# Output projection of a gated-linear mixer with tokens as rows and its layer norm along rows

## The chip, the cores and the metric

One core of one Trainium2 chip runs the whole program in one launch. The metric is the device time in microseconds (us); of several executions the median is given. The engines are TensorE (PE), VectorE (DVE), ScalarE (ACT) and GpSimd (POOL); SyncE (SP) issues the loads of weights.

## What is computed

Batch 1, 256 tokens, width 1024, three mixers and a feed-forward in a first block, then a second block of two layers. The change lies in the second block:

```python
def second_block(x, ...):
    for layer in range(DEPTH_2):
        if layer < N_A_LAYERS:
            y = gla_mixer(x, ...)
        else:
            k_sh, v_sh = shared_kv(x, w_kv)
            y = dilated_mixer(x, ..., k_sh, v_sh)
        x = layer_norm(DEEPNORM_ALPHA * x + y, ln_g[layer], ln_b[layer])
    return x

def gla_mixer(x, w_in, w_a2, b_a2, norm_g, w_out):
    ...
    return (o.astype(x.dtype) * jax.nn.silu(g)) @ w_out

def layer_norm(x, g, b):
    mu = jnp.mean(x32, axis=-1, keepdims=True)
    xc = x32 - mu
    var = jnp.mean(xc * xc, axis=-1, keepdims=True)
    return xc * lax.rsqrt(var + LN_EPS) * g + b
```

Everything is fp32. `ALPHA` is the square root of 2.

## The kernel before, in words

The weights stream from HBM as some 100 chunks of 1 MB, each 1024 rows by 256 columns, in an order fixed by constants: ..., `GG` (4 chunks, the gate of the gated-linear mixer), `GOUT` (4, its output projection), `SK` (3, shared keys), `SV` (3), `SWA` (16, queries and gate of the last mixer), `SOUT` (4, the last projection). SP loads a chunk into one of four raw buffers when its former occupant has been split. ScalarE writes the chunk's rounded high half (`high`), VectorE the remainder (`low`, L997), into one of three buffer pairs, once the chunk three before has been multiplied. PE makes each product as three fp32r products: high by high, low by high, high by low (`three`, L1544 to L1546), 48 of 256 columns for one chunk.

Activations lie with features on the partitions: `x`, `xe`, `tb`, `hhi`, `hlo` are [128, 8, 256], eight blocks of 128 features by 256 tokens. Weights are then the stationary operand (`fm`), and a result bank holds two blocks of features for all tokens. `fm_first` interleaves two chunks over k, so that PE has work while its inputs still arrive. In `SV` and `SOUT` the activations are stationary and the result has tokens as rows.

Each engine runs its own list of instructions in order, with semaphores between them. For every chunk b its list holds the work on the chunk's result and the split of chunk b+3; for the chunks in `LATE` the split comes after all the other work. `RESULT_DRAIN` says by whose count a result bank (three, used in turn) is free again, `CHUNK_MARK` when a chunk has been multiplied.

Around `GOUT` before: VectorE adds each result bank to `xe` (ALPHA times the input of the layer, with features on partitions, made by POOL). After two of four chunks PE takes the mean of those 512 features by products with a matrix of 1/1024 (`shift_mean`), and VectorE subtracts twice that mean. ScalarE squares, POOL adds squares, PE sums them over partitions (`sums`, `rest_mean`, `last_squares`) and then makes 16 warm-up products of the identity (`warm`, L1592). VectorE corrects the mean, finds the root and scales the eight blocks (L1430); ScalarE rounds them to `hhi` with the bias (L657), VectorE writes `hlo` (L1033), POOL two of the blocks. Then SK starts. During `SV`, POOL makes ALPHA times the normed x for the last residual.

Around `SOUT` before: PE adds the last residual itself, by 16 products of a 128x128 block of `x` with the identity (L1934) in front of the real products. ScalarE copies the banks to `z` with row sums (L909, L921), takes squares about a provisional mean with row sums (L916, L922), and VectorE ends the norm along rows (L1452 to L1468) for each tile t of 128 tokens: row scalars in `zs`, parameters repeated on all partitions in `ln_rows`. The first 512 features of a tile give the provisional mean.

Of the kernel before, what the change touches and what calls it, by code (L numbers as in the profile page):

```python
# [89 lines left out]
def results_of(c):  # L90

    if BRANCH <= c < WOUT:
        return 4
    if DOWN <= c < GK:
        return 2 if (c - DOWN) % 3 == 2 else 0
    return 1


def drainer_of(c):

    if c < MISC or BRANCH <= c < WOUT or (UP <= c < DOWN and (c - UP) % 2 == 1):
        return "dve"
    if GOUT <= c < SV or SWA <= c < SWA + 12:
        return "dve"
    return "act"
# [15 lines left out]
for _c in range(NC):  # L121
# [8 lines left out]
    CHUNK_MARK.append(_m)  # L130

# [73 lines left out]
def build(nc, xT, crow_d, cols_d, ident_d, rope1_d, rope2_d, amask_d, cmask_d, tri_d, dmask_d, sel_d, rel_d, w_a2_d,  # L205
          w_ada, wts, ln_rows_d, out_d):
# [3 lines left out]
    with ctx:  # L210
# [17 lines left out]
        ident = sb("ident", [P, P])  # L228
        meanw = sb("meanw", [P, P])
# [37 lines left out]
        result_rows = y[:, :, :].rearrange("p a b -> p (a b)").rearrange("p (t n) -> p t n", t=2)  # L267
        xsw = sq[:, 0:2, :]
# [17 lines left out]
        with ExitStack() as st:  # L286
            xe = sb("xe", [P, KT, T], at=st)
            gq = sb("gq", [P, 4, T], at=st)
            gk = sb("gk", [P, 4, T], at=st)
            alrT = sb("alrT", [16, T], at=st)  # L290
            wa2 = sb("wa2", [16, 512], at=st)
            keep = sb("keep", [P, 1024], at=st)
            cum = sb("cum", [P, 1024], at=st)
            qI = sb("qI", [P, 1536], at=st)
# [7 lines left out]
            with ExitStack() as early:  # L302
                gfacs = sb("gfacs", [P, 4096], at=early)
            gohi = sb("gohi", [P, KT, T], f32r, at=st)
            golo = sb("golo", [P, KT, T], f32r, at=st)
            grs = cum[:, :].rearrange("p (h t) -> p h t", h=4)
# [5 lines left out]
        with ExitStack() as st:  # L312
# [14 lines left out]
            zs = sb("zs", [P, 2, 16], at=st)  # L327
# [10 lines left out]
        rest = pX[:, T:2 * T]  # L338
        msq = pS[:, 0:T]
# [13 lines left out]
        NORMS = ("n1", "n2", "n3", "n4", "n5")  # L353
# [6 lines left out]
        centered, summed = {"n5": sem("n5_centered")}, {"n5": sem("n5_summed")}  # L360
        rows_in, z_shift, z_summed, z_squared, z_var, z_root = (
            sem(n) for n in ("rows_in", "z_shift", "z_summed", "z_squared", "z_var", "z_root"))
        shift_known, rest_squared, var_known, recentered = (
            sem(n) for n in ("shift_known", "rest_squared", "var_known", "recentered"))
        in_lo_pool = {n: sem(f"{n}_lo_pool") for n in ("n3", "n5")}
# [124 lines left out]
        def _(pool):  # L490
# [34 lines left out]
            def presum(n, need):  # L525

                for i in range(2):
                    a = 2 * i + 2
                    pool.wait_ge(squares[n], need[i])
                    if i:  # L530
                        pool.wait_ge(presummed, 2 * ("n2", "n4", "n5").index(n) + 1)
# [11 lines left out]
            for c in range(1, NC + 1):  # L543
# [14 lines left out]
                if c - 1 == SK - 1:  # L558
                    presum("n5", (2, 3))
                    split_lo_pool("n5", x, lambda i: col("ln_b", i))  # L560
                if SV <= c - 1 < SWA:
                    pool.wait_ge(scaled["n5"], KT)
                    rest = [i for i in range(KT) if i not in LO_POOL]
                    for k in rest[2 * (c - 1 - SV):2 * (c - 1 - SV) + 2]:
                        nc.gpsimd.tensor_scalar(x[:, k, :], tb[:, k, :], col("ln_b", k), ALPHA, ALU.add, ALU.mult
                                                ).then_inc(x_ready, 1)
                    if c - 1 == SWA - 1:
                        pool.wait_ge(in_lo_pool["n5"], 2)
                        for k in LO_POOL:
                            nc.gpsimd.tensor_scalar(x[:, k, :], x[:, k, :], ALPHA, None, ALU.mult).then_inc(x_ready, 1)  # L570
# [32 lines left out]
        def _(act):  # L603
# [38 lines left out]
            def norm_guess(n, eps):  # L642

                if n not in centered:
                    act.wait_ge(mean_known[n], 1)
                else:
                    act.wait_ge(var_known, 1 if n == "n5" else 2)
                var = logvar[:, :] if n in centered else stat
                nc.scalar.activation(rstd[:, :], var, ACT.Abs_reciprocal_sqrt, bias=col(eps, 0)).then_inc(guess_known, 1)
# [22 lines left out]

            TAIL = 3
            for c in range(1, NC + 1):
# [4 lines left out]
                if b not in LATE and b != WOUT + 2:  # L679
# [214 lines left out]
                if GOUT < b < SK:  # L894
                    n, j = "n5", b - GOUT
                    for i in ((), (0, 1), (2,), (3,))[j]:
                        act.wait_ge(centered[n], i + 1)
                        nc.scalar.activation(sq[:, 2 * i:2 * i + 2, :], tb[:, 2 * i:2 * i + 2, :], ACT.Square
                                             ).then_inc(squares[n], 1)
                    if j == 2:  # L900
                        load_root()
                if b == SK - 1:
                    norm_guess("n5", "eps5")
                    split_hi("n5", tb, lambda k: col("ln_b", k))
                if SOUT <= b < SOUT + 2:
                    j = b - SOUT
                    ps = result(FIRST_RESULT[b])
                    for t in range(2):
                        nc.scalar.activation(z[:, t, T * j:T * j + T], ps[:, T * t:T * t + T], ACT.Copy,  # L909
                                             accum_out=zs[:, t, j:j + 1]).then_inc(drained_act if t else act_self, 1)  # L910
# [1140 lines left out]
```

## Time and profile before

| | |
|---|---|
| median of 3 runs | 795.97 us (795.43 to 796.54) |
| the profiled execution's own time | 794.63 us |
| its span | 792.8 us |
| PE, DVE, ACT, POOL busy | 93%, 68%, 50%, 15% of the span |
| products of GOUT | 558.33 to 583.53 us |
| products of SK to SWA | from 593.73 us |
| products of SOUT | 761.18 to 784.83 us |

Times inside are microseconds from the start of the span. A row of a timeline gives start, length, engine, line of the kernel, operation, output<-inputs, shapes and count, and in brackets the idle time before it and what ended it. PE's products overlap: their starts tell the pace. An fp32 product (identity, mean) leaves two records, an fp32r product or a transpose one.

### The profile page before, as it was taken

The page shows a single profiled execution, that of the slowest core. Times are in us where ns is not written, and L with a number is a line of the kernel's source. Part 1 is how long each engine was busy: PE and PEld are TensorE (multiplying, and loading weights), DVE is VectorE, ACT ScalarE, POOL GpSimd, SP SyncE. Part 2 cuts the span into 40 slices and gives each one's busy share as a digit, 9 for nine tenths or more (in the row PEclk, how much of TensorE's full clock was granted, in tenths as well). Part 3 has the DMA queues.
Part 4 walks back from the last instruction along what each step waited for, and adds up shares of the span by engine and source line. Part 5 has one row for each costly group of instructions (what it writes and reads, how often), then busy time and mean ns, then how long its engine had stood idle before and what let it go on. Part 6 is the DMA issues. An engine that isn't in the chain of part 4 may idle for free. (4 is left out here: it accounts for less than half of the span.)

```text
span 792.8 us, 14332 instructions
## 1 busy us (share of the span) xinstructions
PE 738.1 (93%) x6028; PEld 722.6 (91%) x6028; DVE 536.8 (68%) x777; ACT 397.3 (50%) x549; POOL 121.2 (15%) x100
## 2 busy tenths in 40 slices
PE   2499999999898999999999999999989999999996
PEld 2399989989898999999999999999989999999995
DVE  4968987675868777777756556926686547556544
ACT  3165645555344554544444337718535556555633
POOL 0030000000421100000001160000025755433000
PEclk9699999999999999999999999979999999999998
DMA  9964656565445256555556614632345653333101
GB/s 353 416 245 174 243 188 258 184 242 212 160 149 223 61 206 212 191 183 177 216 222 236 216 58 164 209 107 93 126 155 208 211 204 117 129 130 111 51 1 54
DMA packets 21096, 140.62 MB, mean 177 GB/s; under 512 B 2372, under 2 KB 3012, under 8 KB 5032
## 3 DMA queue, kind: packets, MB, share of 16 engines
q1 hardware_dynamic: 20600, 137.80, 47.8%
q0 software_dynamic: 432, 1.90, 0.6%
q8 instruction: 48, 0.79, 0.4%
q14 instruction: 16, 0.13, 0.0%
HBM read 138.64 MB, written 1.05 MB: 176 GB/s over the span
## 5 line engine op out<-in xcount | busy, mean ns | idle before, releaser
L1544 PE MATMUL res<-hhi,whi 128*128 128x256 f32 (+1 forms) x1168 | 336.7, 288 | 7.2 <-DVE hlo L1033 5.1
L997 DVE TENSOR_TENSOR wlo<-raw,whi 128x2048 fp32r<-128x2048 f32 (+1 forms) x105 | 236.8, 2257 | 145.9 <-ACT whi L620 141.3
L1545 PE MATMUL res<-hhi,wlo 128*128 128x256 f32 (+1 forms) x1168 | 331.0, 283 | 0.0
L1546 PE MATMUL res<-hlo,whi 128*128 128x256 f32 (+1 forms) x1168 | 331.0, 283 | 0.0
L620 ACT ACTIVATE whi<-raw 128x2048 fp32r<-128x2048 f32 (+1 forms) x105 | 195.8, 1867 | 137.1 <-issue 108.3
L1544 PEld LDWEIGHTS res<-hhi,whi 128*128 128x128 f32 (+1 forms) x1168 | 223.4, 191 | 9.5 <-issue 4.7
L1545 PEld LDWEIGHTS res<-hhi,wlo 128*128 128x128 f32 (+1 forms) x1168 | 223.5, 191 | 0.3
L1546 PEld LDWEIGHTS res<-hlo,whi 128*128 128x128 f32 (+1 forms) x1168 | 223.2, 191 | 0.2
L532 POOL TENSOR_TENSOR sq<-sq 128x512 f32<-128x512 f32 x6 | 14.9, 2482 | 293.9 <-ACT sq L815 168.5
L1544 PE MATMUL res<-uhi,whi 128*128 128x256 f32 x176 | 49.3, 280 | 1.0 <-ACT y L816 1.0
L1545 PE MATMUL res<-uhi,wlo 128*128 128x256 f32 x176 | 49.2, 280 | 0.0
L1546 PE MATMUL res<-ulo,whi 128*128 128x256 f32 x176 | 49.2, 280 | 0.0
L504 POOL TENSOR_TENSOR sq<-sq,rope 128x512 f32<-128x512 f32 x18 | 37.9, 2106 | 72.3 <-ACT sq L635 72.3
L1592 PE MATMUL pS<-ident 128*128 128x128 f32 x242 | 29.6, 284 | 15.3 <-DVE mod L1010 15.3
L1592 PEld LDWEIGHTS pS<-ident 128*128 128x128 f32 x242 | 29.3, 200 | 15.9 <-issue 15.7
L1010 DVE CUSTOM_DVE_ANT_0 raw<-raw,cact,cols 128x1024 f32<-128x1024 f32 x32 | 41.8, 1344 | 0.0
L1544 PE MATMUL res<-whi,hhi 128*128 128x256 f32 x144 | 41.0, 285 | 0.0
L1546 PE MATMUL res<-wlo,hhi 128*128 128x256 f32 x144 | 40.8, 283 | 0.0
L1545 PE MATMUL res<-whi,hlo 128*128 128x256 f32 x144 | 40.7, 283 | 0.0
L1544 PEld LDWEIGHTS res<-uhi,whi 128*128 128x128 f32 x176 | 33.1, 188 | 1.2 <-ACT y L816 1.2
L1545 PEld LDWEIGHTS res<-uhi,wlo 128*128 128x128 f32 x176 | 33.1, 188 | 0.0
L1546 PEld LDWEIGHTS res<-ulo,whi 128*128 128x128 f32 x176 | 33.1, 188 | 0.0
(328 smaller groups left out, 1144.0 us busy)
## 6 DMA issues: line engine op xcount, KB each, us to landing
raw<-in_wts SPq DMA_DIRECT2D x100, 1024.0 KB, 5.0
raw<-in_w_ada SPq DMA_DIRECT2D x16, 1024.0 KB, 4.9
gates<-in_w_ada SPq DMA_DIRECT2D x6, 1024.0 KB, 8.3
raw<-in_wts SPq DMA_DIRECT2D x4, 768.0 KB, 6.1
y<-in_w_ada SPq DMA_DIRECT2D x2, 1024.0 KB, 10.9
x<-in_xT SPq DMA_DIRECT2D x2, 512.0 KB, 6.1
ln_rows<-in_ln_rows POOLq DMA_DIRECT2D x1, 1024.0 KB, 7.5
out<-y SPq DMA_DIRECT2D x4, 256.0 KB, 2.1
```

The costliest lines, as they stand in the source:

```text
L504: nc.gpsimd.tensor_tensor(xsw, xsw, table[:, 1:2, :].to_broadcast([P, 2, T]), ALU.mult).then_inc(sin_done, 1)
L532: nc.gpsimd.tensor_tensor(sq[:, 0:2, :], sq[:, 0:2, :], sq[:, a:a + 2, :], ALU.add).then_inc(presummed, 1)
L620: nc.scalar.activation(hi[:, 0:kt * w], raw[RAW_OF["w", c] % RAW][:, 0:kt * w], ACT.Copy).then_inc(hi_ready, 1)
L997: nc.vector.tensor_tensor(lo[:, 0:b], raw[RAW_OF["w", c] % RAW][:, 0:b], hi[:, 0:b].bitcast(f32), ALU.subtract).then_inc(lo_ready, 1)
L1010: nc.vector.tensor_tensor_reduce(out=w[:, D * i:D * i + D], in0=w[:, D * i:D * i + D], in1=cact[:, :], op0=ALU.mult, op1=ALU.add, scale=1. ...
L1544: mm(out, ah, bh, start=first, stop=False)
L1545: mm(out, al, bh, start=False, stop=False)
L1546: return mm(out, ah, bl, start=False, stop=last)
L1592: mm(pS[:, 512:640], ident[:, :], ident[:, :], start=True, stop=True)
```

## The change

GOUT's products now have the activations as stationary operand, so that their results have tokens as rows. The residual comes first into each bank as products of `xe` with the identity. The first of its four chunks is multiplied for both tiles of 128 tokens, then the three others for tile 0, which is then complete, then the three others for tile 1. The results are five banks instead of four. ScalarE and VectorE norm each tile along rows as in the tail, with parameters that POOL loads into `gv` (`ln_rows5`). The normed rows `x_rows` are turned back by PE, 8 transposes for each tile (`hidden`), into `pS` and `pT`, from which ScalarE and VectorE write `hhi` and `hlo` (`hidden_high`, `hidden_low`). The transposes of tile 0 stand between the last two products of 24. The last chunk of GOUT gets its own split buffers `wgo`. SK is no longer interleaved with SK+1.

`x_rows` is kept. POOL scales it by ALPHA in two steps, and in SOUT VectorE adds it while it empties each bank, with row sums (`row_add`); PE's identity products there and ScalarE's copies are gone, and the squares are taken from `z`.

```diff
-    return 1
+    return 2 if c == SK - 1 else 1
...
-    if GOUT <= c < SV or SWA <= c < SWA + 12:
+    if SK <= c < SV or SWA <= c < SWA + 12 or c >= SOUT:
         return "dve"
...
+CHUNK_MARK[GOUT + 1] = RESULT_MARK[FIRST_RESULT[GOUT + 3]]
+CHUNK_MARK[GOUT + 2] = CHUNK_MARK[GOUT + 3]
...
+            if c == SK - 1:
+                return wgo[:, 0, :], wgo[:, 1, :]
...
-            return SOUT - 1 if c == NC - 1 else c - SPL
+            return {NC - 1: SOUT - 1, SK - 1: GOUT - 1, SK + 2: GOUT}.get(c, c - SPL)
...
+                if c - 1 == GG:
+                    pool.wait_ge(o_done, 2)
+                    pool.dma_start(gv[:, :, :], ln_rows5_d).then_inc(rows5_in, 16)
+                if SV <= c - 1 < SV + 2:
+                    t = c - 1 - SV
+                    pool.wait_ge(h_transposed, 4)
+                    nc.gpsimd.tensor_scalar(x_rows[:, t, :], x_rows[:, t, :], ALPHA, None, ALU.mult).then_inc(x_ready, 1)
...
+            def hidden_high(t):
+                for i in range(2):
+                    act.wait_ge(h_transposed, 2 * t + i + 1)
+                    nc.scalar.activation(hhi[:, 4 * i:4 * i + 4, t * P:t * P + P],
+                                         (pS, pT)[t][:, 512 * i:512 * i + 512].rearrange("p (k n) -> p k n", k=4), ACT.Copy
+                                         ).then_inc(h_hi, 1)
...
+                if b == GOUT + 3:
+                    row_sum(result(FIRST_RESULT[b])[:, 0:T], 1, T, T, 1).then_inc(drained_act, 1)
+                    act.wait_ge(z_shift, 2)
+                    row_squares(z[:, 1, 0:512], 1, 0, 3).then_inc(z_squared, 1)
+                    high(SK)
+                    hidden_high(0)
+                    ps = result(FIRST_RESULT[b] + 1)
+                    row_sum(ps[:, :], 1, 512, 512, 2).then_inc(z_summed, 1)
+                    row_squares(ps[:, :], 1, 512, 4).then_inc(drained_act, 1)
+                    row_root(1, 0)
+                    hidden_high(1)
+                    high(SK + 1)
...
+                if b == GOUT + 3:
+                    dve.wait_ge(drained_act, RESULT_DRAIN[FIRST_RESULT[b]][1])
+                    shift_of(1)
+                    low(SK)
+                    hidden_low(0)
+                    rows_normed(1, 0, gv, x_rows, x_rows_ready)
+                    hidden_low(1)
+                    low(SK + 1)
...
+                if SOUT <= b < SOUT + 2:
+                    ps = result(FIRST_RESULT[b])
+                    own(row_add(ps[:, 0:T], 0, T * (b - SOUT), T, b - SOUT))
+                    row_add(ps[:, T:2 * T], 1, T * (b - SOUT), T, b - SOUT).then_inc(drained_dve, 1)
...
+                    if c == GOUT + 1:
+                        for t in range(2):
+                            ps = bank(r + 1 + 2 * t)
+                            residual(ps, 0, t, (2, 3))
+                            wh, wl = weights(GOUT + 1)
+                            for k in range(KT):
+                                last = token_product(ps, 0, t, k, gohi, golo, wh, wl, False, k == KT - 1)
+                            last.then_inc(product_done, 1)
+                            ps = bank(r + 2 + 2 * t)
+                            residual(ps, 0, t, range(4, KT))
+                            for d in range(2):
+                                wh, wl = weights(GOUT + 2 + d)
+                                for k in range(KT):
+                                    last = token_product(ps, T * d, t, k, gohi, golo, wh, wl, False, d == 1 and k == KT - 1)
+                                if t == 1 and d == 0:
+                                    hidden(0)
+                            last.then_inc(product_done, 1)
+                        warm(16, ident, pX[:, 0:P])
+                        hidden(1)
...
                     if c == SOUT:
-                        pe.wait_ge(x_ready, KT)
-                        first = [bank(r + d) for d in range(3)]
-                        for d in range(2):
-                            for t in range(2):
-                                residual(first[d], T * t, t, (2 * d, 2 * d + 1))
-                        residual(first[2], 0, 0, range(4, KT))
+                        first = [bank(r + d) for d in range(2)]
```

**Where instructions moved.** VectorE before SK, in the kernel before: the rows from the last addition of a result (L1395) through the mean's correction (L1415, L1423) and the root to the first blocks of `hlo` (L1033). SK's first two weight chunks were split ahead of this.

```order
L1395 TENSOR_TENSOR tb<-tb,res 128x512 [waits shift_known,product_done]
L1398 ISA [waits n5_centered]
L1415 COPY sq<-pX 128x256 [waits n5_mean]
L1416 TENSOR_TENSOR rstd<-sq 128x256 [waits dve_self]
L1423 TENSOR_TENSOR tb<-tb,sq 128x512 [waits n5_squares] x2
L1421 TENSOR_TENSOR logvar<-pS,rstd 128x256 [waits rest_squared,n5_mean]
L1423 TENSOR_TENSOR tb<-tb,sq 128x512 [waits n5_squares] x2
L1021 SCALAR_TENSOR_TENSOR sq<-rstd 128x256 [waits guess_known]
L1022 SCALAR_TENSOR_TENSOR sq<-logvar,sq 128x256 [waits dve_self]
L1023 SCALAR_TENSOR_TENSOR rstd<-sq,rstd 128x256 [waits dve_self]
L1430 SCALAR_TENSOR_TENSOR tb<-tb,cols,rstd 128x256 [waits recentered,rstd_known]
L1430 SCALAR_TENSOR_TENSOR tb<-tb,cols,rstd 128x256 [waits recentered]
```

The same place now: tile 1's shift, the split of SK's first chunk (L1016), tile 0's `hlo` from the transposes in `pS` (L1436), then the norm of tile 1.

```order
L1400 TENSOR_SCALAR zs<-zs 128x1 [waits drained_act]
L1401 TENSOR_SCALAR zs<-zs 128x1 [waits dve_self]
L1016 TENSOR_TENSOR wlo<-raw,whi 128x2048 [waits product_done,hi_ready]
L1436 TENSOR_TENSOR hlo<-pS,hhi 128x4x128 [waits h_hi] x2
L1409 TENSOR_SCALAR zs<-zs 128x1 [waits z_summed,z_shift]
L1410 TENSOR_TENSOR zs<-zs 128x1 [waits dve_self]
L1411 TENSOR_TENSOR zs<-zs 128x1 [waits dve_self]
L1413 SCALAR_TENSOR_TENSOR sq<-tb,zs,gv 128x512 [waits z_squared,dve_self]
L1418 TENSOR_TENSOR zs<-zs 128x1 [waits drained_act,dve_self]
L1419 SCALAR_TENSOR_TENSOR zs<-zs 128x1 [waits dve_self]
L1421 SCALAR_TENSOR_TENSOR sq<-tb,zs,gv 128x512
L1424 SCALAR_TENSOR_TENSOR zs<-zs 128x1 [waits z_root,dve_self]
```

The weights' split of SK and the hidden rows of tile 0 now stand between the two tiles' norms, so the norm of tile 1 is queued behind both.

PE at the start of the last projection, before: the last gate product, then identity products that wait for a bank emptied by ScalarE.

```order
L1546 MATMUL res<-hlo,whi 128x256
L1934 MATMUL res<-ident,x 128x128 [waits drained_act,x_ready]
L1934 MATMUL res<-ident,x 128x128 x11
L1544 MATMUL res<-whi,ohi 128x256 [waits d_lo,lo_ready]
L1545 MATMUL res<-whi,olo 128x256
```

Now, the same place:

```order
L1555 MATMUL res<-hlo,whi 128x256
L1553 MATMUL res<-whi,ohi 128x256 [waits lo_ready,d_lo,drained_act]
L1554 MATMUL res<-whi,olo 128x256
L1555 MATMUL res<-wlo,ohi 128x256
L1553 MATMUL res<-whi,ohi 128x256
```

The identity products and their wait are gone from here; the first real product carries the waits.

## Rows read from the trace of the kernel before

**Rows 1.** The page, busy time, share of the span and records of TensorE
```profile
PE 738.1 (93%) x6028; PEld 722.6 (91%) x6028; DVE 536.8 (68%) x777; ACT 397.3 (50%) x549; POOL 121.2 (15%) x100
```

**Rows 2.** PE's waits from 538 us on: who, for whom, us, times, longest
```profile
PE res L1544 <- DVE hlo L1033: 2.2, 1, 2.2
PE res L1934 <- ACT sgs L943: 1.3, 1, 1.3
```

**Rows 3.** Timeline of PE, GOUT to SK: start, length, engine, line, operation, out<-in
```profile
557.84 0.28 PE L1546 MATMUL res<-hlo,whi 128*128 128x256 f32 x1
558.33 0.36 PE L1544 MATMUL res<-gohi,whi 128*128 128x256 f32 x1 [0.21 <-DVE wlo L997]
...
583.53 0.28 PE L1546 MATMUL res<-golo,whi 128*128 128x256 f32 x1
...
593.73 0.36 PE L1544 MATMUL res<-hhi,whi 128*128 128x256 f32 x1 [2.21 <-DVE hlo L1033]
```

**Rows 4.** Timeline of PE, the last projection
```profile
756.96 0.28 PE L1546 MATMUL res<-hlo,whi 128*128 128x256 f32 x1
758.51 2.92 PE L1934 MATMUL res<-ident,x 128*128 128x128 f32 x24 [1.27 <-ACT sgs L943]
761.18 0.37 PE L1544 MATMUL res<-whi,ohi 128*128 128x256 f32 x1
...
778.36 1.05 PE L1934 MATMUL res<-ident,x 128*128 128x128 f32 x8
779.17 0.36 PE L1544 MATMUL res<-whi,ohi 128*128 128x256 f32 x1
...
784.83 0.28 PE L1546 MATMUL res<-hlo,ohi 128*128 128x256 f32 x1
```

**Rows 5.** Timeline of VectorE before the last projection: gated low rows, last weights
```profile
760.50 0.69 DVE L1532 TENSOR_TENSOR olo<-y,ohi 128x512 fp32r<-128x512 f32 x1 [0.69 <-ACT ohi L973]
...
764.52 2.29 DVE L997 TENSOR_TENSOR hlo<-raw,hhi 128x2048 fp32r<-128x2048 f32 x1
```

**Rows 6.** Timeline of VectorE: a tensor_tensor_reduce from PSUM
```profile
743.98 0.69 DVE L1476 CUSTOM_DVE_ANT_0 dsc<-pS,dmask 128x512 f32<-128x512 f32 x1
```

**Rows 7.** Timeline of VectorE and ScalarE in the tail: row norm, summing copy
```profile
782.44 1.41 DVE L1468 SCALAR_TENSOR_TENSOR y<-sq,zs,ln_rows 128x512 f32<-128x512 f32 x2
...
785.87 0.21 DVE L1452 TENSOR_SCALAR zs<-zs 128x1 f32<-128x1 f32 x1 [2.02 <-ACT tb L921]
...
788.92 1.41 DVE L1468 SCALAR_TENSOR_TENSOR y<-sq,zs,ln_rows 128x512 f32<-128x512 f32 x2
...
785.15 0.60 ACT L921 ACTIVATE tb<-res 128x512 f32<-128x512 f32 x1 [3.66 <-PE res L1546]
```

**Rows 8.** The chain that ended last: four transposes of 128x128
```profile
659.06 0.44 PE pT L1721 x4
```

**Rows 9.** Timeline of VectorE (two rows) and ScalarE: last low rows, weights' high half
```profile
563.59 0.69 DVE L1042 TENSOR_TENSOR golo<-y,gohi 128x512 fp32r<-128x512 f32 x1 [0.70 <-ACT gohi L893]
...
593.10 0.48 DVE L1033 SCALAR_TENSOR_TENSOR hlo<-tb,cols,hhi 128x256 fp32r<-128x256 f32 x1 [0.18 <-ACT hhi L657]
...
563.46 1.90 ACT L620 ACTIVATE whi<-raw 128x2048 fp32r<-128x2048 f32 x1
```

**Rows 10.** The chain's last gated-linear output product; the page's load of 1 MB parameters
```profile
538.90 0.22 PE pS L1908 x2
...
ln_rows<-in_ln_rows POOLq DMA_DIRECT2D x1, 1024.0 KB, 7.5
```

**Rows 11.** Timeline of PE from 518 us: narrow products of the gated-linear attention
```profile
517.91 2.17 PE L1891 MATMUL pX<-qI,gfacs 128*48 128x16 f32 x24
```

**Rows 12.** Windows: us, busy of PE, PEld, DVE, ACT, POOL, granted clock, DMA, GB/s
```profile
524.00:526.00 2.00, 2.00 (x11) 1.88 (x10) 1.94 (x11) 0.00 (x0) 0.00 (x0) 0.50 0.00 0
...
528.00:530.00 2.00, 2.00 (x13) 1.89 (x13) 0.00 (x0) 0.00 (x0) 0.00 (x0) 0.90 0.00 0
...
591.00:593.00 2.00, 0.53 (x5) 0.34 (x4) 1.82 (x5) 0.44 (x2) 0.00 (x0) 1.00 0.00 0
```

More of the change, by code:

```diff
@@ L678, in _ @@
                     nc.scalar.activation(alrT[:, :], ps[0:16, 0:T], ACT.Copy).then_inc(drained_act, 1)
-                if b not in LATE and b != WOUT + 2:
+                if b not in LATE and b not in (GOUT + 1, GOUT + 2) and b != WOUT + 2:
                     high(c + 2)
@@ L902, in _ @@
[L902 to L906, printed above, removed]
+                if b == GOUT:
                     ps = result(FIRST_RESULT[b])
                     for t in range(2):
[L909 to L910 removed]
+                        row_sum(ps[:, T * t:T * t + T], t, 0, T, 0).then_inc(drained_act if t else act_self, 1)
@@ L1447, in _, with shift_of, rows_normed @@
-                if b >= SOUT + 2:
-                    t = b - SOUT - 2
-                    g_row, b_row = ln_rows[:, 0, :], ln_rows[:, 1, :]
+                def shift_of(t):
+                    own(nc.vector.tensor_scalar(zs[:, t, 5:6], zs[:, t, 0:1], zs[:, t, 1:2], -1.0 / 512, ALU.add, ALU.mult))
+                    nc.vector.tensor_scalar(zs[:, t, 7:8], zs[:, t, 5:6], 0.5, None, ALU.mult).then_inc(z_shift, 1)
+                def rows_normed(t, base, rows, dst, ready):
+                    g_row, b_row = rows[:, 0, :], rows[:, 1, :]
@@ L1644, in last_squares, with token_product, residual, hidden @@
                 last.then_inc(mean_known[n], 1)
-            def shift_mean(n):
-                src = xe if n == "n5" else x
-                for k in range(4):
-                    pe.wait_ge(summed[n], k // 2 + 1)
-                    last = mm(stat, meanw[:, :], src[:, k, :], start=k == 0, stop=k == 3)
-                last.then_inc(mean_known[n], 1)
-            def rest_mean(n):
-                for k in range(4, KT):
-                    pe.wait_ge(centered[n], k // 2 + 1)
-                    last = mm(rest, meanw[:, :], tb[:, k, :], start=k == 4, stop=k == KT - 1)
-                last.then_inc(mean_known[n], 1)
+            def token_product(ps, at, t, k, ih, il, wh, wl, first, last):
+                return three(ps[:, at:at + T], ih[:, k, t * P:t * P + P], il[:, k, t * P:t * P + P],
+                             wh[:, k, :], wl[:, k, :], first, last)
+            def residual(ps, at, t, ks):
+                for i, k in enumerate(ks):
+                    mm(ps[:, at + P * i:at + P * i + P], xe[:, k, t * P:t * P + P], ident[:, :],
+                       start=at == 0 and i == 0, stop=False)
+            def hidden(t):
+                for i in range(2):
+                    pe.wait_ge(x_rows_ready, 2 * t + i + 1)
+                    for k in range(4 * i, 4 * i + 4):
+                        last = nc.tensor.transpose((pS, pT)[t][:, P * k:P * k + P], x_rows[:, t, P * k:P * k + P], ident[:, :])
+                    last.then_inc(h_transposed, 1)
             def units(s):
@@ L1954, in _ @@
                                 for t in range(2):
-                                    last = token_product(first[d], T * t, t, k, *both[d], k == KT - 1 and t == 1)
+                                    last = token_product(first[d], T * t, t, k, ohi, olo, *both[d], k == 0 and t == 0, k == KT - 1 and t == 1)
                                 if k == KT - 1:
@@ L1960, in _ @@
                             ps = bank(r + 2 + t)
-                            if t:
-                                residual(ps, 0, 1, range(4, KT))
                             for d in range(2):
```

245 lines of the change are left out of this document (100 added, 145 removed).

## The prediction

> **What bounds the kernel now.** I read the page first: TensorE (PE) is busy for 93% of the span [rows 1], so a change is worth what it does to PE's idle gaps and to PE's own work, plus the tail after the last product. The list of PE's waits, from 538 us on, gives the gaps that the change can reach: 2.2 us before the first shared-key product, waiting for the low half of the hidden rows, and 1.3 us before the last projection, waiting for ScalarE's gate drain [rows 2]. The PE timeline around the output projection (chunks GOUT to GOUT+3) shows the stage: the last product of the stage before starts at 557.84, the projection runs from 558.33 to 583.53, and the first product of SK starts at 593.73 [rows 3]. Those last 10.1 us hold statistics, 16 warm-up products and the wait. The timeline of the last projection shows 24 records of identity products (12 products; an fp32 product leaves two records) from 758.51, the first real product at 761.18, 4 more identity products at 778.36, and the last product at 784.83 [rows 4]. One 256-column product costs 0.119 us start to start (144 of them between 761.18 and 778.36); one identity product of x costs 0.2225 us (12 in 2.67 us) [rows 4].
>
> **The last projection (SOUT).** Before, PE asks for three banks at once; the third is released only by the gate drain, so PE idles from 757.08 (756.96 plus one product) to 758.51 and then pays 2.67 us of identity products ahead of the first real one [rows 4]. Now it asks for two banks, whose drains lie chunks back, and has no identity products. The first product moves from 761.18 to about 757.1: **-4.1 us**. Cover: the last pair of gated low rows is written at 760.50 + 0.69 = 761.2 [rows 5] and is first used 72 products later, at 765.7; the last two weight chunks are split by 766.8 [rows 5], needed at 768.5 and 771.4. Nothing takes the place of the wait. The second tile loses its 4 identity products, 779.17 - 778.36: **-0.8 us** [rows 4].
>
> The residual is now added by VectorE while it drains, `tensor_tensor_reduce` of 512. The nearest row is the same instruction on PSUM plus an SBUF table: 0.69 us, plus an accumulator read [rows 6]. Before, ScalarE's summing copy took 785.15 to 785.87 with hand-over [rows 7]; the new one should take 0.8: **+0.1 us** at the tail. Bounds: 0 (the two equal) and +0.4 (the squares, now behind the add, come late; they overlap four small VectorE steps and a 0.75 us one, so I take no wait). The first tile's drain and norm take 5.5 us (778.36 to 782.44 + 1.41 [rows 7]) against 5.7 us of products for the second tile: the cover is 0.2 us thin, and gone it costs a few tenths.
>
> **The gated-linear projection (GOUT).** It gets the 16 identity products that SOUT loses, 16 x 0.2225 = 3.6 us of PE, 8 transposes in its middle (four take 0.44 [rows 8], so 0.9 us), and loses the mean products and two halts. I follow it on the old trace's clock.
> - PE: four identity products from 557.96 to 558.85; PE no longer waits for the second weight chunk (558.33 [rows 3]). One chunk alone uses a pair of k in 1.43 us, so after three pairs, at 563.1, it outruns VectorE: the last pair of low rows is done at 563.59 + 0.69 [rows 9]. A new wait of about 1.3 us; what is queued behind it is everything else on PE. GOUT ends at 565.85.
> - Then 24 products and 2 identities (3.3 us) to 569.15; 48 and 4 (6.6) to 575.75, which completes the first token tile; 3.3 to 579.05; 48, 4 and 8 transposes (7.5) to 586.55. Weights: the split of GOUT+3 now follows GOUT+2 directly (ScalarE 1.90 [rows 9], VectorE 2.29 [rows 5] each), ready at 570.0, used at 572.9. It no longer waits for a product, since it has its own buffer.
> - First tile's norm: same instructions as the tail, 5.5 us [rows 7], so rows ready at 581.25. PE wants them at 582.8, before the last 24 products: 1.5 us to spare.
> - In VectorE's queue then: shift of tile 2 (0.4), ScalarE squares (about 0.9 with hand-overs, estimated from the 0.60 us copy [rows 7]) and high half of SK's weights (1.90), VectorE low half (2.29), low halves of tile 1 (two, 1.3): 588.1. The second tile's sum is there at 586.55 + 0.2 + 0.7 = 587.45, so the queue and not PE starts the second norm, by 0.65 us.
> - Second norm from its first step to the first half row: 785.87 to 788.92 + 0.7, 3.75 us [rows 7], so 591.85. PE's hand-over 0.15 (593.10 + 0.48 to 593.73 [rows 3, 9]) and four transposes 0.44 [rows 8], hand-over to ScalarE 0.2 (784.95 to 785.15 [rows 4, 7]), its copy 0.6 [rows 7], VectorE's subtract 0.7 with its hand-over [rows 9], 0.15 again: SK starts at 594.1. Before: 593.73 [rows 3]. So **+0.4 us**: 3.6 + 0.9 us more PE work and a 1.3 us wait are paid for because the serial piece after the last product shrinks from 10.1 to 7.5 us and the other mean work is gone. Bounds: -1.2 (reads and hand-overs shorter by 5 in 100 over the 18 us chain from 575.75, and no queue delay) and +1.5 (the same the other way, and the strided PSUM reads a third slower). I take the middle, since every piece but the strides has a row.
>
> After SK: one chunk now runs alone for 5.7 us, so SK+1's low half, which stands behind tile 2's in the queue, must be there by 599.8; it is at about 598.3. SP's loads for later chunks follow those splits and have 5 us each. POOL loses two row splits and now scales the rows in two long steps that nobody reads until SOUT; its 1 MB load of the new parameters (7.5 us to land for the like [rows 10]) is issued at 539, when the gated-linear output is there [rows 10], and used at 576. All three cost nothing.
>
> **Sum.** -4.1 - 0.8 + 0.1 + 0.4 = **-4.4 us** on the profiled execution's 794.63, giving 790.2. The median of the runs is 795.97, 1.34 above that execution, so I forecast 795.97 - 4.4 = **791.6**.
>
> **Rivals.**
> 1. *The clock falls before SK.* Now PE's warm-up ends at 590.05, and until 594.1 it has only 0.9 us of transposes: 4 us of near idleness, against 2.3 before. In the trace the granted clock stayed at 1.00 through that shorter pause [rows 12], but it fell to the lower level (1.2 GHz, 0.50) during a stretch of products only 16 columns wide [rows 11], and the full-size products from 524.2 on ran at 11 records in 2 us until the clock came back at about 528.3 [rows 12]. The same here costs half of that 4.1 us: 791.6 + 2.0 = 793.6. For: the pause is longer. Against: it still holds transposes, and is broken three times. Chance 0.2. The Trainium skill (TensorE: Matmul & The Clock Gate, Part 4, PE-mode transpose) says that transposes do not count as PE being busy; by that the whole pause is idle and this rival is the likelier. No run here shows transposes alone.
> 2. *The second norm is not in the queue's hands*: the chain is quicker and PE's last product starts it. That gives about 1.2 us less, 790.4. Chance 0.12; and with the chain slower by 1.1 us, 792.7, chance 0.13.
> 3. *The change does not lift SOUT's wait*, because another wait stands right behind it. Then only 2.67 + 0.8 us of identities go: -2.9, 793.1. Against: the two banks and both weight chunks are ready well before 757 in the program's order. Chance 0.03.
> 4. *Slower: late parameters.* The new load goes behind POOL's wait for the gated-linear output. The first norm stands behind it on VectorE, then the weight split, then PE's transposes with 24 products behind them. Each us past 576.5 is passed on whole, since the VectorE queue is the bound. It ends slower only if the load lands after 581; 10 us late at 586.5 gives 801. Before's load of that size took 7.5 us [rows 10], so a whole 35 us would have to be lost. Chance 0.04.
>
> **Numbers.** Forecast as summed 0.48; rivals 1 to 4: 0.2, 0.25, 0.03, 0.04. The range reaches from 790.0 (quick chain, tail +0) to 794.2 (clock rival with a chain 0.6 slower). A measurement tells about 0.2% (1.6 us) from no change. All cases but the last, and rival 1 stacked on the worst chain, lie over 1.6 us below 795.97: faster 0.9, same 0.05, slower 0.05.
>
> **What would show it.** In the new profile: no identity products and no gap before the last projection; its products from about 4 us earlier relative to SK; a wait of about 1.3 us on low rows at the third pair's end of GOUT; transposes of tile 1 without wait; SK's first product 36.1 us after the last GG product instead of 35.8; the granted clock at 1.00 in the first 5 us of SK. A wait before the mid-product transposes, a wait on the parameter load, or a granted clock under 1 there makes the forecast wrong.

## The result, and the profile after

The changed kernel takes **789.44 us** (median of 7 runs, 787.56 to 793.48) against 795.97 for the kernel before (7 runs, 794.80 to 797.25): ratio 0.9923, 95% interval 0.9901 to 0.9945, so faster by 0.6 to 1.0%. A second set on another occasion (experiment e1) gave 0.9932, interval 0.9918 to 0.9946. The forecast was 791.6 with a range from 790.0 to 794.2: the sign was right, and the time lies 0.56 us below the range.

The two profiled executions are 794.63 and 787.56 us long (spans 792.8 and 785.8). This table splits their 7.0 us by marks on TensorE's (PE's) timeline; a stage ends at the start of its last product plus 0.12 us, the pace of products. "Untouched" is code with the same instructions in both kernels.

```
stretch, us                               before   after   after - before   forecast
start to WOUT's first product (untouched) 218.91  217.47   -1.44             0
WOUT to the narrow products (untouched)   294.15  293.99   -0.16             0
narrow products to last GG product (unt.)  44.90   44.53   -0.37             0
last GG product to SK's first              35.77   35.70   -0.07            +0.4
SK's first to the end of the stage before SOUT
                                          163.35  163.36   +0.01             0
that end to SOUT's first product            4.10    0.00   -4.10            -4.1
SOUT's first to its last product           23.77   22.79   -0.98            -0.8
last product to the end of the span         7.85    7.96   +0.11            +0.1
```

So the stages that the change touches give -5.03 us where -4.4 was forecast, and 1.97 us of the profiles' difference lies ahead of them. The spans are given to 0.1 us, so the last row of the table is known no better than that.

The page after, PE's row, against [rows 1]:

```profile
PE 733.6 (93%) x6020; PEld 718.9 (91%) x6020; DVE 531.8 (68%) x788; ACT 396.6 (50%) x550; POOL 111.1 (14%) x89
```

PE's waits of the kernel after, from 538 us on (who, for whom, us, times, longest), against [rows 2]:

```profile
PE pT L1671 <- DVE x L1429: 1.3, 1, 1.3
PE res L1553 <- DVE golo L1058: 1.1, 1, 1.1
PE pT L1734 <- DVE dp L1494: 1.0, 2, 0.5
PE res L1553 <- DVE hlo L1436: 0.8, 1, 0.8
```

The 1.3 us on the gate drain is gone, as forecast. The new wait on gated low rows (`golo`) is there, with 1.1 us for a forecast 1.3. In place of the 2.2 us before SK stand two waits of the second norm's end, 1.3 for the first half row and 0.8 for the low half.

PE's timeline of the kernel after, GOUT to SK (start, length, engine, line, operation), against [rows 3]:

```profile
555.99 0.38 PE L1663 MATMUL res<-ident,xe 128*128 128x128 f32 x2
...
562.37 0.38 PE L1553 MATMUL res<-whi,gohi 128*128 128x256 f32 x1 [1.08 <-DVE golo L1058]
...
580.79 1.04 PE L1671 MATMUL pS<-ident,x 128*128 128x128 f32 x8
...
584.53 3.73 PE L1601 MATMUL pX<-ident 128*128 128x128 f32 x32
589.53 1.32 PE L1671 MATMUL pT<-ident,x 128*128 128x128 f32 x8 [1.27 <-DVE x L1429]
591.69 0.36 PE L1553 MATMUL res<-hhi,whi 128*128 128x256 f32 x1 [0.84 <-DVE hlo L1436]
```

The first tile's transposes at 580.79 follow the products without a wait. The second tile is complete at 584.53, where the warm-up begins, and SK starts 7.16 us later, against 10.08 before (593.73 - 583.53 - 0.12 [rows 3]). The last GG product ends at 555.99 here and at 557.96 before: take 1.97 us from a time of the prediction to find it in this profile.

PE's timeline of the last projection, against [rows 4]:

```profile
754.93 0.28 PE L1555 MATMUL res<-hlo,whi 128*128 128x256 f32 x1
755.05 0.28 PE L1553 MATMUL res<-whi,ohi 128*128 128x256 f32 x1
...
772.02 0.28 PE L1555 MATMUL res<-hlo,ohi 128*128 128x256 f32 x1
772.14 0.28 PE L1553 MATMUL res<-whi,ohi 128*128 128x256 f32 x1
...
777.72 0.28 PE L1555 MATMUL res<-hlo,ohi 128*128 128x256 f32 x1
```

No identities, no gap, and the second tile's first product 0.12 us behind the one ahead of it, as any other.

VectorE's timeline of the kernel after, around the second norm of the new stage, and in the tail (against [rows 7]):

```profile
577.86 1.42 DVE L1429 SCALAR_TENSOR_TENSOR x<-sq,zs,gv 128x512 f32<-128x512 f32 x2
...
582.27 2.29 DVE L1016 TENSOR_TENSOR wlo<-raw,whi 128x2048 fp32r<-128x2048 f32 x1 [2.69 <-ACT whi L619]
584.48 1.28 DVE L1436 TENSOR_TENSOR hlo<-pS,hhi 128x512 fp32r<-128x512 f32 x2
585.68 0.20 DVE L1409 TENSOR_SCALAR zs<-zs 128x1 f32<-128x1 f32 x1
...
778.03 0.69 DVE L1458 CUSTOM_DVE_ANT_0 tb<-res,x 128x512 f32<-128x512 f32 x1 [0.30 <-PE res L1555]
...
778.85 0.21 DVE L1409 TENSOR_SCALAR zs<-zs 128x1 f32<-128x1 f32 x1
```

And ScalarE's, the queue that feeds it:

```profile
579.62 0.72 ACT L674 ACTIVATE sq<-tb,zs 128x512 f32<-128x512 f32 x1 [1.89 <-DVE zs L1401]
...
580.34 1.90 ACT L619 ACTIVATE whi<-raw 128x2048 fp32r<-128x2048 f32 x1
...
584.73 0.60 ACT L670 ACTIVATE tb<-res 128x512 f32<-128x512 f32 x1 [1.52 <-PE res L1555]
585.22 0.19 ACT L670 ACTIVATION_READ_ACCUMULATOR tb<-res 128x1 f32 x1
```

The second norm starts at 585.68 without any idle time noted before it, right behind the low halves of the first tile, while its sum was read at 585.22 + 0.19 = 585.41. A hand-over follows that reading: in e9 below, where the norm does wait for the sum, it starts 0.80 us after ScalarE began to make it (583.77 to 584.57), which here would be 584.73 + 0.80 = 585.53. So VectorE's queue started the norm and not PE, but only by 0.15 us. Squares, SK's high half, SK's low half (2.69 us waited for) and the low halves stand in one line ahead of it.

Of the 1.97 us ahead of the stage, 1.44 come before WOUT's first product, most of them right in front of it and in code that both kernels have. The kernel before, VectorE and PE:

```profile
216.96 3.50 DVE L1226 SCALAR_TENSOR_TENSOR hlo<-y,hhi 128x512 fp32r<-128x512 f32 x2
...
218.91 0.36 PE L1544 MATMUL res<-hhi,whi 128*128 128x256 f32 x1 [0.94 <-DVE hlo L1226]
```

The kernel after:

```profile
216.63 2.38 DVE L1242 SCALAR_TENSOR_TENSOR hlo<-y,hhi 128x512 fp32r<-128x512 f32 x2
...
217.47 0.36 PE L1553 MATMUL res<-hhi,whi 128*128 128x256 f32 x1
```

The same two instructions took 3.50 us in one and 2.38 in the other, and PE waited 0.94 or not at all. The experiments show whether that belongs to the kernel.

### The profile page after: what moved, and what is told of

Same layout as the page of the kernel before. It is cut to its first block and busy times, and to the rows that moved or that the text cites. A ratio compares the mean times of both kernels' runs of the same rounds, so it can differ in the third digit from the quotient of the medians.

```text
span 785.8 us, 14317 instructions
## 1 busy us (share of the span) xinstructions
PE 733.6 (93%) x6020; PEld 718.9 (91%) x6020; DVE 531.8 (68%) x788; ACT 396.6 (50%) x550; POOL 111.1 (14%) x89
## 5 line engine op out<-in xcount | busy, mean ns | idle before, releaser
L1016 DVE TENSOR_TENSOR wlo<-raw,whi 128x2048 fp32r<-128x2048 f32 (+1 forms) x104 | 233.6, 2249 | 150.5 <-ACT whi L619 146.1
L1601 PE MATMUL pS<-ident 128*128 128x128 f32 x210 | 25.8, 285 | 15.4 <-DVE mod L1029 15.4
L1601 PEld LDWEIGHTS pS<-ident 128*128 128x128 f32 x210 | 25.6, 202 | 15.9 <-issue 15.7
L537 POOL TENSOR_TENSOR sq<-sq 128x512 f32<-128x512 f32 x4 | 10.8, 2697 | 182.2 <-ACT sq L830 168.4
```

Of the source, the lines that this page charges most:

```text
L537: nc.gpsimd.tensor_tensor(sq[:, 0:2, :], sq[:, 0:2, :], sq[:, a:a + 2, :], ALU.add).then_inc(presummed, 1)
L1016: nc.vector.tensor_tensor(lo[:, 0:b], raw[RAW_OF["w", c] % RAW][:, 0:b], hi[:, 0:b].bitcast(f32), ALU.subtract).then_inc(lo_ready, 1)
L1601: mm(to, of[:, :], of[:, :], start=True, stop=True)
```

## The experiments

Ten kernels, in three sets. The kernel before ran beside each set, with medians 795.62 (23 runs), 795.37 (18) and 795.43 (16). Since medians also hold the untouched code, I read each profile by the stretches of the table.

**The changed kernel again (e1).** No edit.

> The changed kernel once more, as the yardstick for the other kernels of this set. Theory A (the change is worth what its two stages show, -5.1 us, and the 1.9 us that the first profile gained before 556 us is chance): median near 791, and the first product of WOUT's chunks and the narrow-product stretch fall differently from profile to profile. Theory B (the 1.9 us belong to the change): median near 789, and the time from the start to the last GG product is again 1.9 us shorter than in the kernel before.

790.29 us (5 runs), ratio 0.9932 (0.9918 to 0.9946). The touched stages repeat to 0.02 us (35.70, 0.00, 22.79, 7.98), but WOUT's first product comes at 218.97 instead of 217.47: **the early time of the first profile doesn't belong to the change.** The delay is another than in the kernel before, though: e1 has no wait at WOUT. It is later already by then, and one difference is the granted clock. Windows of e1 and then of the first profile (columns as in [rows 12]; the granted clock is the third number from the end):

```profile
43.00:45.00 2.00, 2.00 (x11) 2.00 (x11) 1.68 (x1) 2.00 (x2) 1.14 (x5) 0.50 0.04 8
43.00:45.00 2.00, 2.00 (x19) 1.97 (x17) 2.00 (x1) 1.72 (x1) 0.85 (x3) 1.00 0.00 0
```

Nor is the wait at WOUT the old kernel's own: it stands again in the profiles of e4, e6, e7 and e8, which have the changed kernel's code there. In e7:

```profile
220.45 0.36 PE L1553 MATMUL res<-hhi,whi 128*128 128x256 f32 x1 [0.96 <-DVE hlo L1242]
```

**The moved buffers alone (e2).** The kernel before, with `zs`, `gq`, `gk`, `qI` and `keep` where the changed kernel has them:

```diff
-            zs = sb("zs", [P, 2, 16], at=st)
-            gq = sb("gq", [P, 4, T], at=st)
...
+                gq = sb("gq", [P, 4, T], at=early)
...
```

> The kernel before with nothing but the new places of five buffers in on-chip memory (zs, gq, gk, qI, keep). Theory B1 (addresses shift how VectorE and GpSimd meet at WOUT): about -1.5 to -2 us against before, all of it ahead of 556 us. Theory A: within 0.5 us of before in every stage.

795.35 us, ratio 0.9993 (0.9983 to 1.0004): the places of the buffers cost and give nothing.

**The last projection as before (e3).** The changed kernel, with SOUT's 16 identity products, its third bank and ScalarE's summing drains put back:

```diff
-                        first = [bank(r + d) for d in range(2)]
+                        first = [bank(r + d) for d in range(3)]
+                        for d in range(2):
+                            for t in range(2):
+                                residual_rows(first[d], T * t, t, T * d, 2)
+                        residual_rows(first[2], 0, 0, 512, 4)
...
```

> The changed kernel with the last projection as before: PE adds the residual by 16 products of 128 columns (identity by x_rows), asks for three banks first, and ScalarE empties the banks. If the last projection is worth what the trace says: +4.1 (start) +0.8 to 1.0 (second tile) -0.1 (tail) = 4.9 us slower than the changed kernel, so the projection and norm of the gated-linear stage alone come to 0 +- 0.5 against before. If that stage is worth more than the trace shows, this kernel stays over 1 us under before.

794.71 us, ratio 0.9994 (0.9983 to 1.0004). The new gated-linear stage stays (35.70 us from the last GG product to SK, before 35.77) and the last projection is the old one to 0.02 us (4.10 and 23.75). So **the new projection by itself is worth nothing that can be told, and what the change gains comes from what the rows allow SOUT to drop.**

**Three banks asked for at once (e4).** The changed kernel with one number of the old one:

```diff
-                        first = [bank(r + d) for d in range(2)]
+                        first = [bank(r + d) for d in range(3)]
```

> The changed kernel, but PE asks for three result banks before the last projection instead of two; no identity products. If the bank wait is a cost of its own: a wait of 1.3 us on ScalarE's gate drain comes back and the kernel is 1.4 us slower than the changed one. If the wait was only cover for something else (gated low rows, weights), under 0.5 us.

792.45 us (6 runs), ratio 0.9951 (0.9935 to 0.9968). The old wait stands in PE's timeline again:

```profile
760.92 0.36 PE L1553 MATMUL res<-whi,ohi 128*128 128x256 f32 x1 [1.33 <-ACT sgs L962]
```

The stretch to SOUT's first product is 1.49 us instead of 0. Of the 4.10 us, the bank is 1.49, which leaves 2.61 for the identities.

**No warm-up before SK (e5).**

```diff
-                        warm(16, ident, pX[:, 0:P])
```

> The changed kernel without the 16 warm-up products between the last gated-linear product and the transposes of tile 1. The pause before SK is then 7.2 us with 8 transposes. Clock rival: the granted clock shows 0.50 in the windows before or after SK's first product, and SK to SWA take about 2 us longer (165.4 instead of 163.36). If a pause of that kind does not lower the clock: 163.4 and the same total.

792.69 us, ratio 0.9957 (0.9941 to 0.9973). Windows of e5 (start:end, length, busy time and count of PE, PEld, DVE, ACT, POOL, granted clock, DMA share, GB/s); SK starts at 595.05:

```profile
589.00:591.00 2.00, 0.00 (x0) 0.00 (x0) 1.88 (x5) 0.29 (x1) 0.53 (x1) 0.91 0.85 328
591.00:593.00 2.00, 0.57 (x3) 0.57 (x4) 1.86 (x6) 0.00 (x0) 0.00 (x0) 0.50 1.01 385
...
601.00:603.00 2.00, 2.00 (x19) 2.00 (x19) 0.35 (x1) 0.00 (x0) 0.00 (x0) 1.00 0.93 385
```

The last product before the transposes starts at 587.31. The granted clock was at the lower level (0.50, 1.2 GHz) in the window from 591, before the transposes (592.43), and full again in the window from 601, six microseconds into SK. The price: SK to the end of the stage before SOUT took 165.94 us instead of 163.36, and the piece before SK grew by 0.44, together 3.0 us.

**The parameters late (e6).** Their load is issued when the first tile's product is done, not after the gated-linear output:

```diff
-                if c - 1 == GG:
-                    pool.wait_ge(o_done, 2)
+                if c - 1 == GOUT + 2:
+                    pool.wait_ge(product_done, RESULT_MARK[FIRST_RESULT[GOUT + 2]])
```

> The changed kernel with POOL's load of the norm's parameters issued only when tile 0 is complete on PE (18 us before SK) instead of after the gated-linear outputs. It takes 7.6 us to land. Rival 4 of the prediction (everything is passed on whole, the VectorE queue being the bound): the stretch from the last GG product to SK grows from 35.7 by about 7.5 to 43.2, and PE waits before the transposes of tile 0, then again after them. If part of it has cover: under 41.

795.54 us, ratio 1.0003 (0.9990 to 1.0016): the whole gain is gone. VectorE's timeline of e6:

```profile
581.20 0.21 DVE L1409 TENSOR_SCALAR zs<-zs 128x1 f32<-128x1 f32 x1 [11.03 <-DMA gv<-in_ln_rows]
```

The first norm starts 23.42 us after the last GG product, 18.81 in the changed kernel: 4.61 late. The stage takes 40.31 us instead of 35.70: 4.61. **The delay of the first norm is passed on whole**, as rival 4 had it. The clock fell too, here at 598 (0.54 in the window 598 to 600), and cost another 1.5 us behind SK.

**PE's wait filled (e7).** Six of the first tile's ten identity products are done in the wait for the low rows:

```diff
+                            if k == 5:
+                                residual(bank(r + 1), 0, 0, (2, 3))
+                                residual(bank(r + 2), 0, 0, range(4, KT))
...
-                            residual(ps, 0, t, range(4, KT))
+                            if t:
+                                residual(ps, 0, t, range(4, KT))
```

> The changed kernel with six identity products of the residual (banks 2 and 3 of the stage) moved into GOUT's wait for the last pair of low rows. They are 1.33 us and the wait is 1.08. If the whole stage hangs on PE up to tile 0's last product: GG end to SK 35.7 - 1.1 = 34.6, and about 1.1 us less in total than the changed kernel. If the stage hangs on the queue behind tile 0 and on tile 1's last product alike: the same 1.1, since both move; if something else sets SK's start, less.

789.74 us (4 runs), ratio 0.9923 (0.9903 to 0.9942). The `golo` wait is gone from the list, and the stage takes 34.37 us: -1.33. Both identity blocks of the first tile are gone from the chain. With the slower start of the product behind each (0.08, below) they took 0.45 us (563.89 to 564.46, less one product) and 0.89 us (567.18 to 568.19, less one), together 1.34. In the wait they cost nothing: the last pair starts 1.37 us after the product ahead of it, and 1.35 in the changed kernel. The median says nothing here, for WOUT started at 220.45 in this profile.

**No residual in the stage (e8).** Queue or PE? This kernel leaves the layer's x out of its sum.

```diff
-                        for t in range(2):
-                            residual(ps, T * t, t, (0, 1))
...
-                            residual(ps, 0, t, (2, 3))
...
-                            residual(ps, 0, t, range(4, KT))
```

> The changed kernel without the residual in the gated-linear stage (16 identity products left out, so the layer's x is missing from its sum). PE up to tile 0's last product saves 0.45 + 0.89 = 1.3 us (GOUT's own 0.89 fall into the wait for low rows), up to tile 1's last product 2.7 us. Queue-bound second norm (prediction): SK starts 1.3 us earlier, 34.4. PE-bound: 2.5 or more earlier, 33.2.

790.03 us (2 runs), ratio 0.9934 (0.9914 to 0.9954). The stage takes 34.36 us, -1.34, though PE lost 3.6 us of work. That is again the 1.34 us of the two blocks ahead of the first tile's last product, and nothing for those behind it, as the queue-bound case had it. The `golo` wait grew from 1.08 to 1.7, and the wait before the last transposes from 1.27 to 2.60: PE arrived earlier and waited for the same queue. And the clock fell. PE's timeline of e8, then its windows:

```profile
589.58 1.32 PE L1671 MATMUL pT<-ident,x 128*128 128x128 f32 x8 [2.60 <-DVE x L1429]
591.74 0.55 PE L1553 MATMUL res<-hhi,whi 128*128 128x256 f32 x1 [0.84 <-DVE hlo L1436]
```

```profile
590.00:592.00 2.00, 1.15 (x8) 0.71 (x6) 1.28 (x3) 1.66 (x3) 0.00 (x0) 0.71 0.97 410
592.00:594.00 2.00, 2.00 (x10) 2.00 (x10) 0.89 (x2) 2.00 (x2) 0.00 (x0) 0.50 0.13 53
...
598.00:600.00 2.00, 2.00 (x19) 2.00 (x18) 0.00 (x0) 0.00 (x0) 0.00 (x0) 1.00 0.99 418
```

The pause from the last warm-up to SK is 5.0 us here (586.70 to 591.74) and 3.7 in the changed kernel (587.98 to 591.69), with the same eight transposes in it. The rest of the program took 2.6 us more to the last projection (165.98 against 163.36), so the kernel with less work on PE is no faster.

**The queue shortened as well (e9).** e7, and SK's high half ahead of the second tile's first squares, so that it fills ScalarE's 1.89 us wait for their shift:

```diff
+                    high(SK)
                     act.wait_ge(z_shift, 2)
                     row_squares(z[:, 1, 0:512], 1, 0, 3).then_inc(z_squared, 1)
-                    high(SK)
```

> e7_fill with one more edit: ScalarE makes the high half of SK's first chunk before it waits for the shift of tile 1, not after. Queue-bound second norm: VectorE then reaches it before tile 1's sum is there, so PE's last product sets it; the sum is only 0.2 to 0.3 us ahead of the queue, so the stage gets 0.3 shorter: 34.37 - 0.3 = 34.1. If the queue were no bound: 34.4, no change.

**788.65 us** (4 runs), ratio 0.9915 (0.9901 to 0.9930), with the shortest stage of those that leave SK whole: 34.23 us. VectorE's timeline, and ScalarE's sum for the second norm:

```profile
578.63 2.29 DVE L1016 TENSOR_TENSOR wlo<-raw,whi 128x2048 fp32r<-128x2048 f32 x1
...
584.57 0.21 DVE L1409 TENSOR_SCALAR zs<-zs 128x1 f32<-128x1 f32 x1 [2.17 <-ACT tb L670]
...
583.77 0.60 ACT L670 ACTIVATE tb<-res 128x512 f32<-128x512 f32 x1 [2.21 <-PE res L1555]
```

The low half of SK's weights no longer waits, the queue is free 2.17 us before the sum comes, and still only 0.14 us was gained over e7. That is the queue's lead of 0.15 seen from the other side: as soon as it is removed, PE's last product and the sum start the norm. Queue and PE were nearly even.

**SK's first chunk by token tiles (e10).** e9, with the first tile's half of SK in the pause, only 4 warm-ups, and SK+1's high half ahead of the second norm's root:

```diff
-                        warm(16, ident, pX[:, 0:P])
+                        shared_keys(0)
+                        warm(4, ident, pX[:, 0:P])
                         hidden(1)
```

> e9_fill_early, and PE multiplies SK's first chunk by tiles: tile 0's half (48 products of 128 columns) right after the last gated-linear product, in the pause in which it had 16 warm-up products and waits (4 warm-up products are left), tile 1's half after the second transposes; ScalarE makes SK+1's high half ahead of the second root. If 128-column products run at half the time of 256-column ones (0.06): the transposes keep their time and 2.7 us go; total 4 us under the changed kernel, near 786. If weight loads hold them at about 0.1: the first half ends 1 us after the normed rows are there, tile 1's half takes 4.8, and nothing or 0.3 us is won. Granted clock 1.00 throughout in both cases.

788.83 us (11 runs), ratio 0.9931 (0.9911 to 0.9952). PE's timeline of e10, the first tile's 48 products:

```profile
584.97 0.22 PE L1553 MATMUL res<-hhi,whi 128*128 128x128 f32 x1
...
590.28 0.32 PE L1601 MATMUL pX<-ident 128*128 128x128 f32 x1
```

48 products of 128 columns in 5.31 us, 0.111 each, where those of 256 columns take 0.119. Half the columns cost 93% of the time, so the second tile's half pays 5.3 us again behind the norm. The first half and the four warm-ups also hold PE too long: the last transposes start at 591.22, 33.5 us after the last GG product, where those of e9 start at 32.1, and so the second half starts 35.6 us after it, where e9 starts SK at 34.2. From the last GG product to the end of the stage before SOUT it is 198.54 us against 197.60 for e9. PE was never idle long, the clock stayed at 1.00, and it is still 0.94 us slower.

## Why the prediction was right, and where it was wrong

The forecast of 791.6 is 2.2 us above the measured 789.44. The mechanisms held. Two terms were mis-sized, that of the gated-linear stage (+0.4, measured -0.07) and that of the second tile (-0.8, measured -0.98), which makes 0.6 us with the rest. The range had no term for the other 1.5 us.

- **The last projection: right.** -4.1 forecast, -4.10 measured. It splits into 1.49 for the third bank (e4) and 2.61 for the identities, forecast 1.4 and 2.67. Rival 3 (another wait stands behind) fell.
- **The second tile: a term mis-sized by 0.2.** Forecast -0.8, measured -0.98. An identity block costs more than its own time: in the kernel before, the next product stands 0.20 us behind the first one after such a block (761.18 and 761.38, 779.17 and 779.37), where it is 0.12 in a run of products. Two blocks gone are 2 x 0.08 = 0.16.
- **The tail: right**, +0.11 for +0.1. From the last product's start to the norm's first step it is 778.85 - 777.72 = 1.13 us, before 785.87 - 784.83 = 1.04 [rows 4, 7].
- **The gated-linear stage: right mechanism, a term mis-sized.** +0.4 forecast, -0.07 measured. The first tile's rows were to be ready at 581.25 and are at 577.86 + 1.42 + 1.97 = 581.25; the last product was to end at 586.55 and does at 584.53 + 1.97 = 586.50. The failed step is "In VectorE's queue then: ... 588.1": measured 585.68 + 1.97 = 587.65. I had added the lengths of rows, but neighbours overlap: from the squares to the end of ScalarE's high half it is 579.62 to 582.24, 2.6 us, where I had 0.9 + 1.90; SK's low half and the first tile's low halves (the prediction counts the tiles from 1 there) run from 582.27 to the norm's first step at 585.68, 3.4 us, where I had 2.29 + 1.3. From the norm on, 589.53 + 1.97 for the transposes and 593.66 for SK lie 0.5 and 0.4 before the forecast, so nearly the whole error is in that queue.
- **Rival 1, the clock: not in this kernel, but close.** In every profile with this shape the granted clock stayed at 1.00 through the pause. For the kernel after:

```profile
588.00:590.00 2.00, 0.73 (x7) 0.49 (x5) 1.86 (x6) 0.00 (x0) 0.00 (x0) 1.00 0.99 379
590.00:592.00 2.00, 1.15 (x8) 0.76 (x7) 1.28 (x3) 1.71 (x3) 0.00 (x0) 1.00 1.03 428
```

  e8, e6 and e5 show that it falls in pauses of 5.0, 5.5 and 7.7 us with eight transposes in them. Its price was 2.6, 1.5 and 2.6 us, forecast 2.0. The Trainium skill (TensorE: Matmul & The Clock Gate, Part 4, PE-mode transpose) says that a transpose does not count as PE being busy in the same way; by that the changed kernel's whole pause of 3.7 us is idle. The runs don't contradict that, since the clock rode through 3.7 us, but the conclusion that I drew from it, that the rival is then the likelier, was wrong.
- **Rival 2, the norm's starter: between its cases.** The queue led by 0.15 us, not 0.65; e8 and e9 show both sides of that edge.
- **Rival 4, the parameters: didn't occur** (the load is early), and e6 bears out its rule: 4.61 us late, 4.61 us passed on. (By that rule 10 us late is 801.6, and not the 801 of the prediction.)
- **The range: the step that made the number miss.** "The range reaches from 790.0 (quick chain, tail +0)": its lower end held only errors of my terms (which add up to 789.9, with -1.2 for the stage and 0 for the tail). With measured terms the sum is -5.03, 790.9 by the same median, and inside the range. The median of the runs lies 1.5 us lower. Part of that is the draw of the runs: the interval of the ratio on 795.97 us is 788.1 to 791.6, and e1's median of the same kernel, 790.29, lies inside my range. In which stretch the median run was faster no trace shows, but of the two profiles' 7.0 us, 1.97 lie in untouched stretches, and those vary from profile to profile:

```
us                            bef.   after  e1     e2     e3     e4     e5     e6     e7     e8     e9     e10
start to WOUT's first         218.9  217.5  219.0  218.8  219.8  220.0  218.5  220.0  220.5  219.6  217.5  218.8
narrow products to last GG     44.9   44.5   44.6   44.8   43.5   45.9   46.0   43.5   44.9   43.5   44.5   44.5
```

  3.0 and 2.5 us from end to end, and in neither row do the changed kernels stand together. The changed kernel's two medians are 0.85 us apart. A forecast from one profile needs about a microsecond on each side for that (an estimate, made afterwards), which would have put 789.44 inside. The second row is a matter of the clock. In the window 526 to 528 the kernel before shows 11 products at 0.50, like 524 to 526 [rows 12], and the kernel after:

```profile
526.00:528.00 2.00, 2.00 (x16) 1.89 (x15) 0.00 (x0) 0.00 (x0) 0.00 (x0) 1.00 0.00 0
```

  That return at another moment is not the change's: in e7, which has the same code there, the same window stands at 0.50.

**What stays open.** The changed kernel's runs spread more (787.56 to 793.48) than those of the kernel before (794.80 to 797.25), and e10's from 787.21 to 794.30. Their mean granted clock goes along: 0.982 in the fastest run of the changed kernel and 0.971 in the slowest, 0.980 and 0.968 to 0.969 at e10's ends. Where their clock was low longer can't be read, because only one run of each kernel is profiled. The pause before SK is a poor suspect: e3, which has it, spans only 794.34 to 797.18, and e10, which hardly has one, has the widest spread.

## What to carry to other kernels

A residual added by identity products is a bank, a wait and PE time at once: where the rows are drained by an engine with room, let the drain add it, and ask for a bank only where its own products begin. In a chain through two queues, take start-to-start differences from a timeline and not the lengths of rows, and compare when each way reaches the shared step: two ways within 0.2 us of each other mean that shortening one alone gives next to nothing (e8, e9). And give a forecast's range a term for the stretches that nobody touches.

## What the runs showed of the hardware that I had not expected

- **A three-part product of 128 columns is hardly cheaper than one of 256**: 0.111 against 0.119 us start to start (e10). Splitting a chunk by tokens nearly doubles its price, 2 x 5.31 against 5.7 us.
- **A pause can cost time behind its end**: one of 3.7 us with eight transposes kept 1.00, one of 5.0 us with the same eight fell to 0.50 at its end and cost 2.6 us after it.
- **The 1 MB load landed in 5.1 us** when issued at 576 us into an otherwise quiet stretch (e6), where the page lists 7.6 for the same load issued among others.
- **The same VectorE pair took 2.38 or 3.50 us** at WOUT in two profiles, enough for 0.94 us of PE's time, ahead of the stage that was changed. The wait it brings is missing in e1 and there in e7, which have the same code up to that point.
